# Row chunks for the first modulation columns, and half of each token row kept on chip for the routed experts, in a float32 hybrid encoder layer

## What is computed

```python
m = silu(c) @ w_ada + b_ada        # (9, 6*1024): shift1, scale1, gate1, shift2, scale2, gate2
h = x * (1 + scale1) + shift1
P = h @ w_in                       # q/k/v, alpha, beta, z; RWKV r/k/v and low-rank w/a/g; merge gates
A = gated_delta_net(P)             # short conv, chunked delta rule, gated norm
B = rwkv7(P)                       # token shift, vector decay, state update, gate
u = sigmoid(P_gA) * (A @ p_a) + sigmoid(P_gB) * (B @ p_b)
x = LN(alpha * x + (1 + gate1) * (u @ w_o))
h2 = x * (1 + scale2) + shift2
y = shared_swiglu(h2) + sum over 8 of 64 experts of gate_e * swiglu_e(h2)
x = LN(alpha * x + (1 + gate2) * y)
```

## Time and profile before

| | |
|---|---|
| three timed runs | 1582.16, 1588.79, 1589.51 us (median 1588.79) |
| the profiled execution | 1585.12 us, span 1583.4 us |
| busy | TensorE 79%, VectorE 33%, ScalarE 15%, GpSimd 8% of the span |
| DMA | 330.77 MB, 209 GB/s over the span |
| chain that ended last | TensorE 69%, DMA 10%, VectorE 8%, issue 7% |

### The profile page before, as it was taken

The page is one execution under the profiler, slowest core; times in us unless marked ns, Lnnn a source line. Parts: engine busy times, 40 slices in busy tenths (PEclk is TensorE's granted clock), DMA queues, the critical chain, the costliest instruction groups (busy, mean ns, idle before and its releaser), DMA issues.

```text
span 1583.4 us, 17565 instructions
## 1 busy us (share of the span) xinstructions
PE 1254.4 (79%) x7270; PEld 711.3 (45%) x7270; DVE 526.1 (33%) x1142; ACT 237.5 (15%) x468; POOL 130.2 (8%) x190
## 2 busy tenths in 40 slices
PE   4898999677766898888897987887888788778446
PEld 1545546367534865875444533333333333333112
DVE  0432467645673533523226411311111111111007
ACT  2122341121002212121001211010011101100000
POOL 6000000110000300300000011111111111110000
PEclk7798899768887898889987988998898989888668
DMA  9356510300104001002445249999999999999555
GB/s 321 128 192 222 198 54 1 79 8 1 53 0 124 12 27 56 27 0 103 163 137 232 101 181 415 413 397 410 406 403 403 409 400 403 407 405 396 247 226 197
DMA packets 96512, 330.77 MB, mean 209 GB/s; under 512 B 20045, under 2 KB 37025, under 8 KB 69546
## 3 DMA queue, kind: packets, MB, share of 16 engines
q1 hardware_dynamic: 84230, 301.60, 49.2%
q0 software_dynamic: 9504, 25.18, 4.1%
q10 hardware_dynamic: 2692, 2.79, 0.6%
HBM read 314.75 MB, written 24.22 MB: 214 GB/s over the span
## 4 chain that ended last, share of the span: by engine, by line
PE 69%; DMA 10%; DVE 8%; issue 7%; SPq 3%; ACT 2%; POOL 0%; POOLq 0%; ACTq 0%; DVEq 0%
PE bank L2169 16%; PE bank L1656 9%; PE bank L2150 6%; DMA ring<-in_we_up_dram 6%; PE bank L1779 5%; PE bank L2044 3%; PE bank L2012 3%; DVE inv L1013 2%; SPq L552 2%; PE bank L2263 2%; DVE ring L1013 2%; PE bank L2124 2%; PE bank L1841 2%; DMA ring<-in_w_in_dram 1%; PE bank L1711 1%
## 5 line engine op out<-in xcount | busy, mean ns | idle before, releaser
L2169 PE MATMUL bank<-ring,rwp 128*64 128x512 f32 (+1 forms) x816 | 281.5, 697 | 122.8 <-issue 122.8
L2169 PEld LDWEIGHTS bank<-ring,rwp 128*64 128x64 f32 (+1 forms) x816 | 87.9, 158 | 288.2 <-issue 288.2
L1656 PE MATMUL bank<-hT,ring 128*128 128x384 f32 x416 | 147.7, 520 | 6.0 <-DVE hT L1013 4.6
L1022 DVE SCALAR_TENSOR_TENSOR seq_cols<-seq_cols,slot_gate,bank 128x256 f32<-128x256 f32 x33 | 22.1, 670 | 371.3 <-ACT seq_cols L734 371.3
L2169 PE MATMUL bank<-MT,rwp 128*64 128x512 f32 (+1 forms) x272 | 143.7, 689 | 0.0
L2150 PE MATMUL bank<-inv,rwp 128*64 128x512 f32 (+1 forms) x408 | 122.1, 616 | 9.0 <-DMA inv<-in_we_down_dram 9.0
L1656 PEld LDWEIGHTS bank<-hT,ring 128*128 128x128 f32 x416 | 84.4, 204 | 67.0 <-issue 11.9
L1779 PE MATMUL bank<-hT,ring 128*128 128x384 f32 x256 | 88.2, 503 | 10.3 <-DMA ring<-in_w_in_dram 10.3
L487 POOL DMA_INDIRECT hT<-h_rows,slot_ids x33 | 33.7, 1020 | 704.0 <-PE bank L2124 449.9
L734 ACT ACTIVATE seq_cols<-bank 128x256 f32<-128x256 f32 x36 | 13.8, 384 | 400.2 <-PE bank L2169 385.0
L1779 PEld LDWEIGHTS bank<-hT,ring 128*128 128x128 f32 x256 | 49.8, 198 | 43.5 <-DMA ring<-in_w_in_dram 10.3
(11 more groups left out here) (371 smaller groups left out, 1743.0 us busy)
## 6 DMA issues: line engine op xcount, KB each, us to landing
ring<-in_we_gate_dram SPq DMA_DIRECT2D x51, 1024.0 KB, 13.6
ring<-in_we_up_dram SPq DMA_DIRECT2D x51, 1024.0 KB, 16.7
inv<-in_we_down_dram SPq DMA_DIRECT2D x51, 1024.0 KB, 10.4
ring<-in_w_ada_dram SPq DMA_DIRECT2D x12, 2048.0 KB, 14.4
MT<-in_we_gate_dram SPq DMA_DIRECT2D x17, 1024.0 KB, 17.3
MT<-in_we_up_dram SPq DMA_DIRECT2D x17, 1024.0 KB, 20.1
qkv<-in_we_down_dram SPq DMA_DIRECT2D x17, 1024.0 KB, 8.5
ring<-in_w_in_dram SPq DMA_DIRECT2D x7, 2048.0 KB, 9.1
```

The lines of the kernel that those rows point to most:

```text
L1656: last = mm(bank[4 + n % 4][:, 0:T], ring[:, u, k, tok(c)], hT[:, k, :], start=(k == 0), stop=(k == KC - 1))
L2169: last = mm(gu[cols, :], hgT[:, n % 2, k, cols], gate_up(gu_slot[w_slot(e)], k), start=(k == 0), stop=(k == KC - 1))
```

## The change

- The first 2048 modulation columns are read in row chunks: eight chunks of 128 rows x 2048 columns with 8 KB rows, two chunks to a DMA in `ring` slots 0 and 1, three in `inv`, one in `F13`. `ada_first(k)` runs four matmuls for a chunk, one for each 512 columns, and accumulates over k in bank 3; the four blocks come out in the four groups of rows. One eviction and one turn (against columns of `ident`) replace four of each.
- `cT` moves to `aT` and is widened to 32 columns with zeros, so that all 128 rows of a modulation's bank are written and one eviction takes them.
- SP issues: four chunks, three chunks, the tokens, the last chunk, the first w_in block. The past rows' 26 loads go to ScalarE's queue; five row loads of ScalarE's go behind its share of the modulation.
- The prompt's tokens are turned in pairs of column blocks and modulated by ScalarE, eight activations with scale and bias from `modT`; VectorE does the third tile, and after it copies the past rows, which stood ahead.
- The level masks are built in `states` rather than in `inv`.
- `h_rows` becomes two tensors of 512 columns; only the first is gathered in the loop, rows of 2 KB. The other half of `h2_tok` stays in SBUF, and `turn_in` picks its columns with twelve matmuls against the one-hot matrix, of which there are three now (`hots`, the third in `modT`). GpSimd's gather waits for all six stores instead of three.
- `decay`, `bonus_in`, `kb` and `F_ready` become one counting semaphore `rw_prep`, `gdn_in` and `rwkv_in` one `state_in`.

```diff
+        cT = flat(aT, 32 * KC).rearrange("p (k r) -> p k r", r=32)
+        ada_k = [flat(ring, 2048, 2048 * i) for i in range(4)]
+        ada_k += [flat(inv, 2048, 2048 * i) for i in range(3)] + [flat(F13, 2048)]
...
-        RING_SEQ = [("ada", i) for i in range(N_ADA1)]
+        RING_SEQ = [("ada_k", 0), ("ada_k", 1)]
...
-            fill(flat(MT, RING * 512, 1024), 0.0)
+            fill(cT, 0.0)
...
-            for n in range(RING):
-                ring_load(n)
+            ring_load(0)
+            ring_load(1)
+            load(flat(inv, 6144).rearrange("p (k n) -> p k n", k=3), w_ada_v[:, 4:7, 0:512 * N_ADA1], "ada_in")
             load(xs[:, 0:2, :], x_prompt[0].rearrange("(t p) d -> p t d", p=P), "x_in")
             load(xs[:, 2, :], x_sample.rearrange("s t d -> (s t) d"), "x_in")
...
+            load(ada_k[7], w_ada_v[:, 7, 0:512 * N_ADA1], "ada_in7")
+            ring_load(2)
...
-                for j in range(4):
-                    rows = slice(32 * j, 32 * j + 9)
-                    f(mod_part[rows, n % RING, :], ada_bank(n)[rows, :], ACT.Copy,
-                      "ada_row" if j == 3 else "act_chain", hold=False)
+                f(mod_part[:, n % RING, :], ada_bank(n)[:, :], ACT.Copy, "ada_row", hold=False)
...
+            act.wait_ge(S("mod_ev"), 1)
+            for k in range(KC):
+                if k % 2 == 0:
+                    act.wait_ge(S("x_turned"), k // 2 + 1)
+                f(hT[:, k, 0:SEQ], bank[X_BANK[k // 2]][:, SEQ * (k % 2):SEQ * (k % 2) + SEQ], ACT.Identity,
+                  "hT_a", hold=False, scale=modT[:, 8 + k, 0:1], bias=modT[:, k, 0:1])
...
+            def ada_first(k):
+                for n in range(N_ADA1):
+                    last = mm(bank[3][32 * n:32 * n + 32, :], cT[:, k, :], ada_k[k][:, 512 * n:512 * n + 512],
+                              start=(k == 0), stop=(k == KC - 1))
...
+            pe.wait_ge(S("hT"), 2)
+            pe.wait_ge(S("hT_a"), KC)
             pe.wait_ge(S("past_ev"), 2)
-            turn_x([0, 2, 3, 4, 6, 7], "x_turned")
-            pe.wait_ge(S("hT"), 6)
...
-                for k in range(KC):
-                    last = tr(bank[k // 4][:, tok(k % 4)], xt[:, n % 3, tok(k)], ident[:, :])
+                for k in range(4):
+                    tr(bank[0][:, tok(k)], xt[:, n % 3, tok(k)], ident[:, :])
+                for k in range(4):
+                    for t in range(TILES):
+                        last = mm(bank[1][:, tok(k)], h2_tok[t][:, 512:D][:, tok(k)], hots[n % 3][:, t, :],
+                                  start=(t == 0), stop=(t == TILES - 1))
                 sig(last, "r_turn")
```

More of the change, by code:

```diff
@@ L927, in _ @@
             for t in range(3):
-                load(h_rows[tok(t), :], h2_tok[t], "h_out")
+                for j in range(2):
+                    load(h_rows[j][tok(t), :], h2_tok[t][:, 512 * j:512 * j + 512], "h_out")
             for j in range(3):
@@ L1465, in spread @@
             def spread(n):
-                hot = onehot[:, n % 2]
+                hot = hots[n % 3]
                 if n < N_PAIR:
@@ new lines, in _ @@
+            for i in range(2):
+                ring_wait(i)
+                ada_first(2 * i)
+                ada_first(2 * i + 1)
+            pe.wait_ge(S("par_in"), 16 * 8)
+            pe.wait_ge(S("pool_chain"), n_const[0])
+            tr(bank[5][:, 256:366], par_a, ident[0:110, 0:110])
+            sig(tr(bank[5][:, 366:386], par_b, ident[0:20, 0:20]), "start_t")
+            pe.wait_ge(S("ada_in"), 16)
+            for k in range(4, 7):
+                ada_first(k)
+            pe.wait_ge(S("x_in"), 32)
@@ new lines, in _ @@
+            for i in range(4):
+                for k in (2 * i, 2 * i + 1):
+                    for t in range(2):
+                        last = tr(bank[X_BANK[i]][:, SEQ * (k % 2) + P * t:SEQ * (k % 2) + P * t + P],
+                                  xs[:, t, tok(k)], ident[:, :])
+                sig(last, "x_turned")
+            turn_x(X_BANK, "x_turned", [2])
+            pe.wait_ge(S("ada_in7"), 16)
+            ada_first(7)
+            pe.wait_ge(S("ada_row"), 1)
+            pe.wait_ge(S("start_ev"), 2)
```

152 lines of the change are left out of this document (78 added, 74 removed).

## The result

The changed kernel takes **1540.15 us** (median of four runs, 1537.54 to 1543.04) against 1589.15 for the kernel before beside it: a ratio of 0.970, 95% interval 0.966 to 0.974. The prediction said 1562, with a range from 1548 to 1578; the sign was right, and the gain was about twice the one forecast.

A forecast was written before the change was run, and what follows sets the result against it. The routed loop was taken as bound by DMA, TensorE work free until its 3.11 us idle is used. Terms -10.5 - 4.8 + 5.65 - 15.3 = -25.0 on 1585.1 gave 1560.1; on the runs' median 1563.8, stated 1562, range 1548 to 1578.

The forecast's parts named there:

- Part 1: Start up to the first projection: begins at 47.7 us against 58.20, -10.5 us, kept within -8 to -13.
- The gate: At the start, TensorE waits after the first four row-chunks for GpSimd's constants, forecast to end at 28.1 us.
- VectorE's tail: Before the first projection: VectorE does the third token tile, then four copies of past rows, 4.4 us.
- The rival of a start gated elsewhere: At the start, low clock or slower loads put the first projection at 54; total -18, about 1568; chance 0.10.
- Part 2: Other modulation columns: one eviction shortens the two-modulation chain to 5.8 us; third gap -2.8, fourth -2.0, together -4.8.
- Nothing is won there: First two modulation gaps: a 2 MB load of 8.74 us ends as late as the chain, so no gain.
- Part 3: Entering the routed loop: twelve picking matmuls replace four transposes per task; together +5.65 us, bounds +3.5 and +8.
- Part 4: Steady routed loop: half gather saves 0.53 us a task over 29 gathers, -15.3 us; bounds 0 and -18.
- some of that comes back: Routed loop: less idle time recovers some of gate-and-up's low-clock time, 8.78 us against 7.09; no amount given.
- That a half gather costs as much as a whole one: Routed loop: engines pay by packet or DMA, so the loop gains 0; -9.7 in all, about 1577; chance 0.12.
- The rule from the Trainium skill: Routed-loop gather: GpSimd DMA takes "2.0 + bytes / 436e3" us, so 2.9 falls only to 2.5; loop -5, total 1572.
- TensorE as the bound: Routed loop, turn ahead of gate-and-up: TensorE becomes the limit, losing 4 us a task; 1599 at 18.2 a task; chance 0.06.

The follow-up runs named there:

- the kernel with late parameters: Changed kernel with the parameters' transposes, which wait for all GpSimd constants, moved behind the other chunks and token transposes; 1533.14 us, ratio 0.967 to the kernel before.
- the run with half rows alone: Kernel before, gathering half rows without picking matmuls, the first half turned twice and the second half of inputs left out; 1572.57 us, ratio 0.990.

## Why the prediction was wrong, point by point

**Part 1, up to the first projection: right in its order, 1.8 us too small.** The gate (GpSimd's constants at 28.1) came at 28.2. The terms that were cautious: 4.3 for the token transposes, which took 3.0 at a clock of 0.93; 1.3 for the last chunk, which took 1.04; 1.4 for the turn, 1.10. VectorE's tail took 4.7, not 4.4. The rival of a start gated elsewhere did not come; but the wait for the constants, which the forecast counted as given, was worth 6.6 us by itself, as the kernel with late parameters shows.

**Part 2, the other modulation columns: the step that failed most, -4.8 against -16.9.** The chain of two modulations came out at 5.38, near the 5.8 forecast, so the third and fourth gap gave -3.25 and -2.44. Two things were not in the sum. "Nothing is won there", said of the first two gaps, was wrong: they fell by 1.4 and 1.55, since the loads landed sooner (why is open). And the blocks behind the gaps were taken at the same length, although part of each had run at a low clock: 12.72 for half a block where the high clock needs 10.5. What the fourth block, the third and the small matmuls gained, 2.15, 3.0 and 2.55 us, is more than the waits of the gaps that were forecast. That the wider evictions alone do this is shown for the fourth block. The 3.0 of the third are not theirs: in the other seven kernels with the new start this block took 22.5 to 23.4 us in place of 20.84, and the small matmuls 8.5 to 9.45 in place of 6.91, so most of the 5.5 is luck of this one trace. From the first projection to the end of the small matmuls it has 111.35 us, those seven 112.8 to 115.4; the kernel before has 127.20, the seven others with the old evictions 124.6 to 126.0. Some 4 us of the 16.9 are thus the choice of the two traces, and the forecast falls short without them too.

**Part 3, entering the loop: +4.3 against +5.65**, within its bounds. The turns were sized well: 4.88 us for the first (5.1 forecast, its picks 3.77) and 3.31 for the second (3.3). The first gather landed 0.8 us sooner and not 0.3; and the turns behind the third, which the sum left out, cost 2.2 each, but ahead of task 3 TensorE then waits 1.5 us for weights in place of 6.7.

**Part 4, the steady loop: -22.3 against -15.3, two errors that partly cancel.** The bytes were taken too dear: half a row was put at 0.53 us a task, from the queue's 12.0% of one stretch; over the 28 tasks that queue has 11.1%, which by the same working gives 0.48, and the run with half rows alone shows 0.39 (0.17 MB less in a task, 0.43 us at 405 GB/s). And the work of TensorE was taken as free, where with half rows it was a gain: 0.26 us a task with useless transposes, 0.27 with the picks. With less idle time the clock stays up, gate-and-up ends sooner, SP issues the next weights sooner, and the DMA engines run dry less often. Another 0.12 came only behind the new start, and its cause is open. TensorE's busy time went from 14.1 us a task to 15.0 and not to 16.55, since gate-and-up fell from 8.7 us on average to 7.4. The prediction saw the low clock of the gate-and-up matmuls (8.78 and 7.09 side by side) and said that "some of that comes back", but gave it no price, on the ground that DMA was the bound. DMA at 1.00 was read as a fixed rate; it was 405 GB/s with dry stretches in it, and the engines did 414 after the change.

**The rivals.** That a half gather costs as much as a whole one is refuted by the halves and quarters with eight transposes: 17.44, 17.05, 16.82 us, all at 404 to 406 GB/s, so the loop pays by bytes. The rule from the Trainium skill that was weighed there, DMA: Bandwidth & Descriptors, Anatomy of one DMA, would have left the loop at -5 by an estimate; the half rows alone gave 0.39 times 28, -11, against -12 by their bytes at 405 GB/s, so at most a small share of that fixed part can be time of the engines here. TensorE as the bound came only two steps further on, with whole rows kept.

## What to carry to other kernels

A DMA-bound loop whose loads are issued when TensorE is done can still pay for TensorE's low clock (here with half rows, not with whole ones): look at the chain for gate matmuls that are longer behind an idle stretch and for loads issued right after them, and price these dry stretches before you call the work on TensorE free. When a gap between matmul blocks is cut, price the block behind it too, at the clock that it will then find. A wait that a change puts early in an in-order queue (here all constants for two small transposes) can cost half of what the change wins there, 6.6 us beside 12.3; ask for each what really needs it.

## What was not expected of the hardware

Useless transposes made a DMA-bound loop faster: sixteen more in a task, 1.7 us of work at 0.11 each, took it from 17.05 to 16.79 us and the flow from 404 to 411 GB/s. The same kind of extra work did nothing where whole rows were gathered (17.40 to 17.46 us in six kernels, whatever the clock), and the 2 MB blocks of the projection landed 1.6 us sooner behind the new start than behind the old, not by ring slot, queue of the small loads or evictions. The cause of either is open.
